# Expert picking in a decoder-layer kernel: three small steps of fourteen lists go from VectorE to ScalarE, the expert rows are spread anew, and the border of two stages and the first head are written in another order

## The reference, cut to what matters

```python
q = (t @ w_query).reshape(n_tok, 8, 2, 64)
s = einsum('thcd,hcnd->thcn', q, sub_keys)        # two score lists of 128 keys
v1, i1 = top_k(s[:, :, 0], 16); v2, i2 = top_k(s[:, :, 1], 16)
cand = v1[..., :, None] + v2[..., None, :]        # 256 candidates
best, j = top_k(cand, 16)
e_idx = take(i1, j // 16) * 128 + take(i2, j % 16)
gate = softmax(best)
out  = sum_k gate_k * gelu(t . expert_u[e_idx_k]) * expert_v[e_idx_k]
```

## Time and profile before

| | us |
|---|---|
| median of three runs | 1978.28 |
| the profiled execution, device time | 1980.26 |
| its span in the trace | 1978.3 |
| TensorE busy | 1952.8 (99%) |
| VectorE busy | 1684.4 (85%) |
| ScalarE busy | 1120.0 (57%) |
| GpSimd busy | 726.5 (37%) |

### The profile page before, as it was taken

How to read it: one execution, slowest core, us unless ns; L and a number is a source line. 1 busy time by engine, 2 the same in 40 slices (tenths; PEclk the granted TensorE clock), 3 DMA queues, 4 the chain that set the end, 5 groups by cost and what they waited for, 6 DMA issues and landing times. The chain is left out here.

```text
span 1978.3 us, 32483 instructions
## 1 busy us (share of the span) xinstructions
PE 1952.8 (99%) x11706; PEld 1736.7 (88%) x11706; DVE 1684.4 (85%) x2368; ACT 1120.0 (57%) x1585; POOL 726.5 (37%) x406
## 2 busy tenths in 40 slices
PE   8999999999999999999999999999999999999999
PEld 8899989999888888999999999999777777777776
DVE  7777778776878677999999999988888888888887
ACT  7665556555676455666565655645455555555454
POOL 0301111011000001888888888886222232222220
PEclk9999999999999999999999999999999999999999
DMA  6745554565455556999999999999899999999997
GB/s 233 244 162 200 199 193 160 187 205 191 150 179 181 191 183 219 322 312 329 321 323 335 333 302 337 331 394 390 330 375 382 367 373 372 379 382 376 376 383 253
DMA packets 137574, 566.48 MB, mean 286 GB/s; under 512 B 44008, under 2 KB 52080, under 8 KB 88112
## 3 DMA queue, kind: packets, MB, share of 16 engines
q1 hardware_dynamic: 87456, 415.09, 57.6%
q0 software_dynamic: 49776, 148.44, 22.1%
q10 hardware_dynamic: 288, 2.36, 0.3%
HBM read 548.30 MB, written 16.88 MB: 286 GB/s over the span
## 5 line engine op out<-in xcount | busy, mean ns | idle before, releaser
L452 DVE TENSOR_TENSOR wlo<-raw,whi 128x1024 fp32r<-128x1024 f32 x242 | 296.1, 1232 | 114.7 <-PE psum L607 72.6
L873 PE MATMUL psum<-xr,whi 128*128 128x384 f32 x2048 | 380.9, 337 | 1.7 <-ACT whi L458 1.7
L896 PE MATMUL psum<-whi,xr 128*128 128x512 f32 x1512 | 364.4, 390 | 2.9 <-DVE xr L1795 1.9
L873 PEld LDWEIGHTS psum<-xr,whi 128*128 128x128 f32 x2048 | 351.1, 188 | 2.4 <-ACT whi L458 2.2
L458 ACT ACTIVATE whi<-raw 128x2048 fp32r<-128x2048 f32 x168 | 320.9, 1910 | 36.7 <-DMA raw<-v_rows 20.6
L896 PEld LDWEIGHTS psum<-whi,xr 128*128 128x128 f32 x1512 | 283.1, 188 | 65.6 <-DVE xr L1795 2.6
L603 PE MATMUL psum<-xr,whi 128*128 128x512 f32 x1296 | 330.3, 397 | 0.1
L445 ACT ACTIVATE whi<-raw 128x1024 fp32r<-128x1024 f32 x244 | 250.0, 1053 | 96.9 <-PE psum L593 42.7
L1330 POOL DMA_INDIRECT arena<-v_rows,small x64 | 145.4, 2272 | 401.1 <-DVE arena L1759 398.4
L603 PEld LDWEIGHTS psum<-xr,whi 128*128 128x128 f32 x1296 | 232.4, 189 | 43.9 <-issue 0.3
L1335 POOL DMA_INDIRECT gates<-arena x96 | 219.9, 2291 | 29.2 <-issue 28.9
(11 more groups left out here) (284 smaller groups left out, 3252.2 us busy)
## 6 DMA issues: line engine op xcount, KB each, us to landing
raw<-stream SPq DMA_DIRECT2D x244, 512.0 KB, 3.3
raw<-v_rows SPq DMA_DIRECT2D x85, 1024.0 KB, 7.7
raw<-u_cols SPq DMA_DIRECT2D x84, 1024.0 KB, 6.5
arena<-v_rows SPq DMA_DIRECT2D x43, 1024.0 KB, 7.6
arena<-u_cols SPq DMA_DIRECT2D x42, 1024.0 KB, 5.5
gates<-arena POOLq DMA_DIRECT2D x8, 1536.0 KB, 9.6
small<-gates SPq DMA_DIRECT2D x62, 192.0 KB, 8.2
arena<-x_t SPq DMA_DIRECT2D x4, 544.0 KB, 6.9
```

What stands on the lines that cost most here:

```text
L452: nc.vector.tensor_tensor(wlo[:, k % 2 * HALF:(k % 2 + 1) * HALF], raw[:, s * HALF:(s + 1) * HALF], f(whi[:, s * HALF:(s + 1) * HALF]), AL ...
L873: mm(bank(at, 0, 2 * TD), hi_w[:, c * P:(c + 1) * P], z_all[:, :, c, 0:TD // TS, :], start=c == 0, stop=False)
L896: last = mm(at[:, (b * 4 + j * 2 + n) * 512:(b * 4 + j * 2 + n + 1) * 512], weights, src, start=begin, stop=end, skip_group_check=True)
```

## The change

For lists t of 2 and more (`FIRST_SHARED = 2`) three VectorE instructions go to ScalarE: the scaling of the key indices becomes two activations in `scale_indices(t)`, the token's offset and the division by the sum become one each in `route_picks(t)`. VectorE's multiplication in m = 7 now waits for the semaphore `idx_scaled`, and for `picked` of the list before. `picked`, which SyncE and GpSimd wait for, is raised by ScalarE. `scale_indices(t-1)` stands in `route_scores(t)` ahead of the copy of the scores (list 15 has a place of its own), `route_picks(t)` in the turn after VectorE's m = 8.

The row products come every 4.2 steps up to row 47 and every 3 after it, in place of every 4.5 up to row 45 and every 2.5 after it.

At the border to the value blocks, the sum of the last two expert blocks is made one by one, the first of them a turn earlier, and the first value block does all products of its first banks and of the 64-row part before those that need the last bank. In the first head, two conversions of constants move on ScalarE from block 1 to block 0, VectorE makes `wf_lo` before the square sums, the clamp `min(z, 0)` and the lambda difference go elsewhere, and the first long reciprocal (L1519) goes one half block forward.

```diff
-            if n < 46:
-                return 6 + n * 9 // 2
+            if n < 48:
+                return 6 + n * 21 // 5
             if n < ROWS:
-                return 211 + (n - 46) * 5 // 2
+                return 207 + (n - 48) * 3
...
+            def scale_indices(t):
+                b = 1 - t % 2
+                for c in range(2):
+                    last = A(idxs[:, c, :], idxu[:, c, :], ACT.Copy, scale=coef[b][:, c:c + 1])
+                last.then_inc(idx_scaled, 1)
+
+            def route_picks(t):
+                h, b = t // 2, 1 - t % 2
+                at = mixed[h][:, 0, :] if b else pick_at[h]
+                gate = mixed[h][:, 1, :] if b else pick_gate[h]
+                act.wait_ge(gate_norm, t - FIRST_SHARED + 1)
+                A(at.bitcast(U32), index, ACT.Identity, bias=token[b])
+                A(gate, gate_exp, ACT.Copy, scale=gate_sum[:, 1:2]).then_inc(picked[b], 1)
+
             def route_scores(t):
                 act.wait_ge(scores_sb, t // 2 + 1)
                 act.wait_ge(sc_taken, t + 1)
+                if t > FIRST_SHARED:
+                    scale_indices(t - 1)
                 A(sc, st[:, t // 2, 1 - t % 2, :, :], ACT.Copy).then_inc(sc_ready, 1)
...
                         route_gates(t)
+                    if t == ROUTES - 1 and n == route_at(t, 3) // 2 + 1:
+                        act.wait_ge(sc_taken, ROUTES + 1)
+                        scale_indices(t)
+                    if n == (route_at(t, 7) + 3) // 2 + 1:
+                        route_picks(t)
...
-                    V.tensor_tensor(idxs, idxu, spread(coef[b].unsqueeze(2), 2, TOPK), ALU.mult)
+                    if t < FIRST_SHARED:
+                        V.tensor_tensor(idxs, idxu, spread(coef[b].unsqueeze(2), 2, TOPK), ALU.mult)
...
                 if m == 7:
+                    if t >= FIRST_SHARED:
+                        dve.wait_ge(idx_scaled, t - FIRST_SHARED + 1)
+                    if t > FIRST_SHARED:
+                        dve.wait_ge(picked[1 - b], (t + 1) // 2)
                     ch.link(V.tensor_tensor(eq, eq, spread(idxs.unsqueeze(1), 1, TOPK), ALU.mult))
                     ch.link(V.tensor_reduce(index, eq.rearrange("p k c m -> p k (c m)"), AX.X, ALU.add))
-                    at = mixed[h][:, 0, :] if b else pick_at[h]
-                    V.tensor_scalar(at.bitcast(U32), index, token[b], None, ALU.add)
+                    if t < FIRST_SHARED:
+                        at = mixed[h][:, 0, :] if b else pick_at[h]
+                        V.tensor_scalar(at.bitcast(U32), index, token[b], None, ALU.add)
                 if m == 8:
                     gate = mixed[h][:, 1, :] if b else pick_gate[h]
                     dve.wait_ge(best_exp, t + 1)
-                    ch.link(V.reciprocal(gate_sum[:, 1:2], gate_sum[:, 0:1]))
-                    V.tensor_scalar(gate, gate_exp, gate_sum[:, 1:2], None, ALU.mult).then_inc(picked[b], 1)
+                    if t < FIRST_SHARED:
+                        ch.link(V.reciprocal(gate_sum[:, 1:2], gate_sum[:, 0:1]))
+                        V.tensor_scalar(gate, gate_exp, gate_sum[:, 1:2], None, ALU.mult).then_inc(picked[b], 1)
+                    else:
+                        V.reciprocal(gate_sum[:, 1:2], gate_sum[:, 0:1]).then_inc(gate_norm, 1)
...
             for n in range(B_U):
                 if n and n % 2 == 0:
                     expert_sums(n - 2)
+                if n == B_U - 1:
+                    expert_sum(n - 1)
...
             weight_lo(0)
-            expert_sums(B_U - 2)
+            expert_sum(B_U - 1)
```

More of the change, by code:

```diff
@@ L343, in hybrid_layer @@
         ROUTES = 2 * HEADS
+        FIRST_SHARED = 2
         LO_SPLIT = B_U - 24
@@ L417, in hybrid_layer @@
             sem("head_scores_ready"), sem("head_scores_taken"), sem("head_best_ready"), sem("head_best_exp"))
+        idx_scaled, gate_norm = sem("key_indices_scaled"), sem("gate_sum_inverted")
         padding_set = sem("padding_set")
@@ L904, in value_block @@
                 part(0, 0, psum, Whi[q][:, 0:P], False, first, False)
-                if first:
-                    pe.wait_ge(bank_free, 2 + F_V)
-                part(0, 1, psum, Whi[q][:, 0:P], False, first, False)
+                if not first:
+                    part(0, 1, psum, Whi[q][:, 0:P], False, False, False)
                 pe.wait_ge(w_lo, base + c + 1)
                 if first:
+                    part(0, 0, psum, Wlo[q][:, 0:P], False, False, False)
                     pe.wait_ge(row_used, ROWS)
-                if residual is None:
+                    for j in range(2):
+                        part(1, j, psum, Wboth[q], False, True, False)
+                    pe.wait_ge(bank_free, 2 + F_V)
+                    for weights in (Whi[q], Wlo[q]):
+                        part(0, 1, psum, weights[:, 0:P], False, weights is Whi[q], False)
+                elif residual is None:
                     for j in range(2):
                         part(0, j, psum, Wlo[q][:, 0:P], False, False, False)
-                        part(1, j, psum, Wboth[q], False, first, False)
+                        part(1, j, psum, Wboth[q], False, False, False)
                 else:
@@ L1004, in token_factor @@
                 hi_half(act, 0, 4)
+                act.wait_ge(loaded, 16)
+                for name in exact:
+                    last = A(exact[name], C[name], ACT.Copy)
+                last.then_inc(means_exact, 1)
                 act.wait_ge(ms_done, 1)
@@ L1070, in head @@
                         hi_half(act, 0, 7)
[L1071 to L1074, removed]
                     if first and p == 2:
@@ L1397, in square_sum @@
             def square_sum():
+                dve.wait_ge(wf_split, 1)
+                V.tensor_tensor(wf_lo, wf, f(wf_hi), ALU.subtract).then_inc(wf_rest, 1)
                 square_pair(2)
                 ch.link(V.tensor_tensor(x_sq[:, 0], x_sq[:, 0], x_sq[:, 2], ALU.add))
-                dve.wait_ge(wf_split, 1)
-                V.tensor_tensor(wf_lo, wf, f(wf_hi), ALU.subtract).then_inc(wf_rest, 1)
                 ch.link(V.tensor_tensor(x_sq[:, 0, 0:2], x_sq[:, 0, 0:2], x_sq[:, 0, 2:4], ALU.add))
@@ L1428, in forget_gates, with lambda_difference @@
                 V.tensor_tensor(a_, a_, z, ALU.min).then_inc(forget_abs, 1)
-            def forget_sums():
-                z, a_, e_, l_ = (fg[n][0:HEADS, :] for n in range(4))
+                dve.wait_ge(forget_abs, 1)
+                ch.link(V.tensor_scalar(z, z, 0.0, None, ALU.min))
+            def lambda_difference():
                 dve.wait_ge(lam_exp, 1)
@@ L1434, in forget_sums @@
                 ch.link(V.tensor_scalar(neg_lam, scal[:, 6:7], -1.0, -LAM_INIT, ALU.mult, ALU.add))
+            def forget_sums():
+                z, a_, e_, l_ = (fg[n][0:HEADS, :] for n in range(4))
                 dve.wait_ge(forget_e, 1)
-                ch.link(V.tensor_scalar(z, z, 0.0, None, ALU.min))
                 ch.link(V.tensor_tensor(z, z, l_, ALU.subtract))
@@ L1509, in head @@
                             forget_gates()
+                        if first and (p, j) == (5, 0):
+                            lambda_difference()
                         if not first and (p, j) in ((2, 0), (4, 0)):
@@ L1516, in head @@
                             forget_sums()
-                        if (p, j) == ((3, 1) if first else (3, 0)):
+                        if (p, j) == (3, 0):
                             dve.wait_ge(head_std, i * 2 + 1)
@@ L1795, in weight_lo, with expert_sum @@
                 V.tensor_tensor(Wlo[q], W[:, chunk, :], f(Whi[q]), ALU.subtract).then_inc(w_lo, 1)
+            def expert_sum(n):
+                dve.wait_ge(half_done, 2 * F_U + 2 * n + 2)
+                dve.wait_ge(low_part, n + 1)
+                V.tensor_tensor(W[:, n, :], bank(U_BANKS[n % 4], 0, TD), W[:, n, :], ALU.add).then_inc(bank_free, 1)
             def expert_sums(n):
```

## The result

The changed kernel takes 2008.32 us (median of 4 runs, 2006.3 to 2008.77) against 1978.1 us before (median of 4 runs): ratio 1.0151, 95% interval 1.0138 to 1.0165, so 30 us or 1.5% slower. The forecast was 2002 us, within 1987 to 2013.

The account below looks back on a forecast made before the run. TensorE's gaps were taken as the only time to be had, with VectorE nearly full: 1980.26 + 20.7 + 8.0 + 1.4 - 3.5 - 0.6 - 2.1 = 2004.2 us, 2002.2 by the median; range 1987 to 2013.

Parts of the forecast that it names:

- The bound and the direction: Whole kernel: only TensorE's gaps count, VectorE at 97% in the picking passes hold-ups on; 1.2% slower, chance of slower 0.90.
- The added wait: VectorE's multiplication in m = 7 waits for ScalarE's two activations in 12 lists, 0.8 to 4.2 us, sum 32 us.
- What reaches TensorE: Expert blocks behind the waits: by fixed distances from the block's start, TensorE waits 0.7 to 3.3 us each, 20.7 together.
- What follows: Expert blocks after each wait: VectorE's lead is zero, so next long turns cost TensorE 8 us more, between 0 and 13.
- the 6 already there: Existing gaps of the knock-on kind, 3.6 us listed, about 6 with those too short to list, subtracted from 14.
- SyncE: Weight loads behind SyncE's wait for `picked` go out up to 3 us late, 7 times: 1.4 us, between 0 and 14.
- The gains: Late expert blocks, border and first head: waits of TensorE go, -3.5, -0.6 and -2.1 us.
- late blocks: Expert blocks after the picking: with rows every 3 steps, waits of 1.8 and 1.7 us go: -3.5, between -5 and +1.
- the head: First head: three waits go, -3.3 us, with 1.2 given back for the next reciprocal: -2.1, between -3.3 and +1.
- the value blocks: Border to the value blocks: the 0.6 us wait for the expert sum is covered by six matmuls: -0.6, between -0.8 and 0.
- The rule on offloading: Picking: the skill's advice for a saturated VectorE, by which the no-waits rival, near 1970 us, would be the outcome; chance 0.04.

Follow-up runs that it names:

- scale_early: The changed kernel with the two index-scaling activations two to three turns earlier on ScalarE: 1970.29 us, ratio 0.9956 to the kernel before.
- picks_only: The changed kernel with the scaling back on VectorE, offset and division staying on ScalarE: 1972.15 us, ratio 0.997 to the kernel before.
- rows_only: The kernel before with the new spacing of the row products alone: 1975.63 us, ratio 0.9988.
- share_only: The kernel before with only the picking shared as in the change: 2008.11 us, ratio 1.0158.
- no_share: The changed kernel with nothing of the picking shared, VectorE doing all 16 lists: 1973.14 us, ratio 0.998 to the kernel before.
- head_only: The kernel before with the changes of the first head alone: 1974.41 us, ratio 0.9982.
- early_and_zeros: The kernel with the scaling early, plus the accumulator's zero fill moved to the second value block: 1968.78 us, ratio 0.9949 to the kernel before.
- rows_aside: The changed kernel with four row products moved ahead of the waiting multiplication of lists 2, 9, 12, 14: 1996.5 us, ratio 1.0089 to the kernel before.

## Why the prediction was right

*The bound and the direction.* TensorE is the only engine whose gaps count, and VectorE's fullness passed every hold-up on. Right: shown by the changed kernel's waits and by `scale_early`, which differs in the place of two activations.

*The added wait.* Forecast from the two rows in each list: 12 waits, 32 us, up to 4.2. Measured: 13, 32.5 us, up to 4.4. List 12 waits as well, since VectorE arrives earlier there than it did. Two scalings take 0.39 us to the next start (817.02 - 816.63), I took 0.35. From the start S of the block named in the prediction the multiplication starts at S + 4.56 without a Gelu and S + 4.98 with one (list 5 alone at S + 5.35), some 0.17 us later than forecast.

*What reaches TensorE.* The gaps in the blocks behind the waits were forecast as 3.3 us for lists 2, 9 and 14, 2.9 for 12, and 0.7 or 1.1 for the others, 20.7 in all. Measured: 3.4 each, 3.0, and 0.8 to 1.6; 23.0 in all. The later start of the multiplication, 13 times 0.17 us, is nearly all of these 2.3 us. The fixed distances from the block's start made this step the safest of all.

*What follows.* The knock-on gaps are 7.0 us, where I had 14 less the 6 already there. I counted too much lead as lost: behind the waits of lists 2, 9 and 11 to 14 no further gap comes. (Behind four of these six TensorE runs at half its clock, which gives VectorE time to catch up; that this is the reason is argued, not tested.) The 6 us were no reading either: the 3.6 us of the earlier trace rows are all the idle time there is, short gaps included. The idle time of the stretch grew by 26.4 us (30.0 - 3.6), where the forecast's two terms give 28.7.

*The failed step: a gap costs its length.* I priced gaps at what they last. The blocks got 41.2 us longer, while the idle time grew by 26.4. The other 14.8 us are mostly TensorE at half its clock: it fell six times, behind the gaps of 3.0 to 3.4 us of lists 2, 9, 12 and 14 and behind two of 1.8 us (lists 6 and 10), and the blocks there are 13.5 us longer than usual block and gap together. The other 14 gaps cost 0.3 us each beyond their length, 3.8 us, about as much as such small losses already made in the kernel before (7.7 - 3.6 = 4.1). The mean granted clock is 0.991 to 0.994 in all four runs of the changed kernel and 0.995 to 1.000 in the runs of the kernel before beside the experiments, so it is no chance of one trace. Nothing in the forecast stood for it. No gap of 3.4 us was in the rows it was made from, but its trace did have the clock at 0.5 twice, unread.

*SyncE.* Forecast 1.4 us, up to 14. `picks_only` shows no cost, though the wait is real, 34 us in 7 places there.

*The gains.* Forecast 6.2 us, in the trace 12.8: late blocks 6.4 (3.5 forecast), which either of two things clears alone, the new rows (`rows_only`) or the lengthened stretch (`share_only`, with the old rows); the head 4.0 (2.1 forecast); the value blocks 2.4 (0.6 forecast). Of the last, the border makes at most 0.8; the rest is one wait at the first row sum, 1.9 us before and 0.7 after, which varies from trace to trace. That wait is the longest of the trace before; the prediction names 1.8 us as the largest and has no term for it:

```profile
PE psum L896 <- DVE xr L1795: 1.9, 1, 1.9
```

The whole stretch, 595.5 and 593.1 us here, lasted 596.8 and 592.1 us in the two traces of the kernel with the scaling early, so its 2.4 us are no shown gain.

The head's gain is partly the clock again: in the trace before it was at 0.5 for 3.4 us twice between 530 and 735 us, in that of the changed kernel never before the expert blocks. Of the traces without such a stretch there, `rows_only` and `share_only`, with the old head, start their expert blocks at 780.65 and 780.64 us, and the changed kernel, `no_share`, `head_only` and `early_and_zeros`, with the new one, at 779.25, 779.76, 778.15 and 777.52: the change in the head is worth 1 to 3 us by that, some 2 us, as forecast.

*Luck.* The blocks lost 11.1 us more than forecast (41.2 for 20.7 + 8.0 + 1.4 = 30.1), the rest gained 6.6 us more (12.8 for 6.2), partly by chance. So the net, 28.5 us in the spans for the forecast's 23.9, is nearer than its parts.

*The rule on offloading.* The Trainium skill, Perfetto Trace Analysis, "Optimizing Scalar/DVE Operations", says moving work from a full VectorE to ScalarE may make sense. This case leans that way without showing it: `scale_early` has 0.9956 and `no_share` 0.998, with intervals that overlap. Where the result is waited for, the same move cost 30 us.

## What to carry to other kernels

Before work is moved to an idle engine, find the instruction that will wait for it, and read from the trace when each of the two gets there: the engine's free time did not tell it here, what stood ahead of the moved work in the same turn did. Measure the way from a fixed event (here the end of a block) along both engines; if it leads past the deadline, the loss is forced whatever slack the averages show. And where TensorE is the bound, look at the granted clock beside the gaps: a gap of 3 us or more cost 1.6 to 3.2 us beyond its length here, the next block included, and when four of them were made shorter (`rows_aside`), the blocks gained 14.4 us for 7.9 us less waiting.

## What the runs showed of the hardware

In the thirteen traces of this case, past the first head, TensorE was granted 1.2 instead of 2.4 GHz (0.50 in the stretches), for 3.4 to 10.2 us, behind each of the 13 gaps of 3.03 us and more. Behind the 16 gaps of 1.76 to 2.05 us it fell 7 times, three of these with no other gap of 1 us or more in the 30 us before. One gap of 1.3 us in the heads, near 535 us, is in all thirteen traces; behind it the clock fell in six. So a gap of 3 us always cost the clock here, a shorter one by what looks like chance.

The price, read in the value blocks: a gap of 0.6 to 2.05 us with the full clock costs itself and 0.2 us, and 0.4 us in the next block. One of 3.6 to 8.6 us, with the lower clock, costs itself and 1.6 to 1.8 us, and from 4.05 us on 0.7 to 1.2 us in the next block. In the expert blocks, one of 1.81 us with the lower clock cost itself and 1.4 us, where 0.3 us is usual.
